# Three narrow products in place of one double-width and one narrow product, and gelu straight from the bank, in the expert up passes of a two-block transformer kernel

## The reference, cut to what matters

```
q = (x @ w_q).reshape(B, S, 8, 2, 128)
s = einsum('bshpk,hpnk->bshpn', q, sub_keys)          # scores of 2 x 128 sub-keys
top_s, top_i = top_k(s, 16); best_s, pos = top_k(cand_s, 16)
g = softmax(best_s);  ids = take_along_axis(cand_i, pos)
u = take(expert_u, ids);  act = gelu(einsum('td,tkd->tk', x, u)) * g
v = take(expert_v, ids);  out = einsum('tk,tkd->td', act, v)
h = x + out;  return rms_norm(h, final_norm_g)
```

## Time and profile before

| | |
|---|---|
| Time, median of 3 executions | 2957.54 us (2951.92 to 2960.43) |
| The profiled execution, its own time | 2955.81 us |
| Its span, first to last instruction | 2954.5 us |
| TensorE busy | 2911.7 us (99%) |
| VectorE busy | 2139.5 us (72%) |
| ScalarE busy | 1570.7 us (53%) |
| Mean granted TensorE clock | 0.997 of full |

### The profile page before, as it was taken

One profiled execution on the slowest core, in us unless ns is written; L12 is line 12 of the kernel. 1 busy time (PEld: TensorE's weight loads), 2 busy tenths in 40 slices (PEclk: granted clock), 3 DMA queues, 4 the chain that ended last, 5 costly groups with the idle time before them and its releaser, 6 DMA issues.

```text
span 2954.5 us, 45739 instructions
## 1 busy us (share of the span) xinstructions
PE 2911.7 (99%) x18502; PEld 2631.0 (89%) x18502; DVE 2139.5 (72%) x3352; ACT 1570.7 (53%) x2406; POOL 419.0 (14%) x304
## 2 busy tenths in 40 slices
PE   9999999999999999999998999999999999999998
PEld 7888888888888888899898999999999999999997
DVE  5566566666666455676589889778999777999776
ACT  4467755555555443577444556444556444556534
POOL 0011101111111000143020000232010133110131
PEclk9999999999999999999999999999999999999999
DMA  7544445555556554654564555788666788666784
GB/s 259 177 151 152 156 177 186 185 186 187 185 186 222 190 198 143 221 177 170 208 211 171 190 183 203 270 302 298 230 236 227 247 306 302 234 232 239 272 310 168
DMA packets 99009, 631.53 MB, mean 214 GB/s; under 512 B 11376, under 2 KB 12784, under 8 KB 31216
## 3 DMA queue, kind: packets, MB, share of 16 engines
q1 hardware_dynamic: 80368, 561.49, 54.3%
q0 software_dynamic: 18432, 67.12, 6.3%
HBM read 623.32 MB, written 4.19 MB: 212 GB/s over the span
## 4 chain that ended last, share of the span: by engine, by line
PE 78%; DMA 9%; DVE 8%; ACT 3%; issue 2%; SPq 0%; ACTq 0%; DVEq 0%
PE ps L292 26%; PE ps L293 13%; PE ps L1406 6%; PE ps L314 6%; PE ps L316 6%; PE ps L315 6%; DMA ring<-in_u_rows_dram,idx 5%; DMA ring<-in_v_rows_dram,idx 4%; PE ps L1408 3%; DVE loR L274 3%; PE ps L305 2%; PE ps L304 2%; PE ps L303 2%; ACT hiR L266 1%; PE ps L1311 1%
## 5 line engine op out<-in xcount | busy, mean ns | idle before, releaser
L274 DVE TENSOR_TENSOR loR<-raw,hiR 128x1024 fp32r<-128x1024 f32 x1017 | 1255.0, 1241 | 621.9 <-ACT hiR L266 618.4
L266 ACT CAST hiR<-raw 128x1024 fp32r<-128x1024 f32 x1026 | 1074.4, 1051 | 803.3 <-PE ps L1408 324.3
L292 PE MATMUL ps<-XA,hiR 128*128 128x448 f32 (+1 forms) x3936 | 1343.9, 391 | 10.7 <-DVE loR L274 9.3
L293 PE MATMUL ps<-XA,loR 128*128 128x224 f32 (+1 forms) x3936 | 1069.3, 272 | 0.0
L292 PEld LDWEIGHTS ps<-XA,hiR 128*128 128x128 f32 x3936 | 739.7, 188 | 127.1 <-DVE loR L274 6.6
L293 PEld LDWEIGHTS ps<-XA,loR 128*128 128x128 f32 x3936 | 747.7, 190 | 0.6
L1406 PE MATMUL ps<-hl,hiR 128*128 128x448 f32 x2048 | 651.0, 377 | 6.2 <-DVE loR L274 5.9
L1408 PE MATMUL ps<-hl,loR 128*128 128x224 f32 x2048 | 543.5, 265 | 0.0
L1406 PEld LDWEIGHTS ps<-hl,hiR 128*128 128x128 f32 x2048 | 385.2, 188 | 42.8 <-DVE loR L274 9.2
L1408 PEld LDWEIGHTS ps<-hl,loR 128*128 128x128 f32 x2048 | 392.1, 191 | 0.2 <-issue 0.2
L1447 POOL DMA_INDIRECT ring<-in_u_rows_dram,idx x64 | 103.2, 1612 | 716.8 <-DVE ring L1469 664.8
(11 more groups left out here) (307 smaller groups left out, 3490.1 us busy)
## 6 DMA issues: line engine op xcount, KB each, us to landing
raw<-in_u_dram SPq DMA_DIRECT2D x128, 1024.0 KB
raw<-in_v_dram SPq DMA_DIRECT2D x128, 1024.0 KB
raw<-in_w_up_dram SPq DMA_DIRECT2D x86, 1024.0 KB
raw<-in_w_down_dram SPq DMA_DIRECT2D x43, 1024.0 KB
raw<-in_w_in_qk_dram SPq DMA_DIRECT2D x32, 1024.0 KB
raw<-in_w_out_dram SPq DMA_DIRECT2D x32, 1024.0 KB
raw<-in_w_in_dram SPq DMA_DIRECT2D x24, 1024.0 KB
raw<-in_w_in_v_dram SPq DMA_DIRECT2D x16, 1024.0 KB
```

The source lines that it names most:

```text
L266: e.copy(hiR[:, r:r + 2, :], raw[n % NR][:, q:q + 2, :]).then_inc(S("hi"), 1)
L274: e.tensor_tensor(loR[:, r:r + 2, :], raw[n % NR][:, q:q + 2, :], hiR[:, r:r + 2, :].bitcast(F32), ALU.subtract).then_inc(S("lo_pool" if p ...
L292: e.matmul(both, wh, X.hl[:, :, k, 0:nt], start=(k == 0), stop=False, skip_group_check=True)
L293: m = e.matmul(dst[:, 0:nt], wl, X.h[:, k, 0:nt], start=False, stop=(k == KC - 1), skip_group_check=True)
```

## The change

A new function `narrow` takes the place of `wide` in the up passes of the experts: for each k three products of 224 columns, hi x h, hi x l, lo x h, into the first half of the bank. `act_u_part` and `dve_u_sum` are gone; `act_gelu` reads the bank and is placed where the copy was (s = 4i+5). TensorE waits for `s_gelu` where it waited for `u_sum`. Beside this some semaphores are merged (`sp_g` for three, `xsq` for two, `gp` for `gp` and `ident`). TS stays 32.

```diff
+    def narrow(e, g, q, X, dst, nt):
+        wait_piece(e, g)
+        hi, lo = hiR[:, g % NQ, :], loR[:, g % NQ, :]
+        for j in range(4):
+            k = 4 * q + j
+            wh, wl = hi[:, j * 128:(j + 1) * 128], lo[:, j * 128:(j + 1) * 128]
+            e.matmul(dst, wh, X.h[:, k, 0:nt], start=(k == 0), stop=False)
+            e.matmul(dst, wh, X.l[:, k, 0:nt], start=False, stop=False)
+            m = e.matmul(dst, wl, X.h[:, k, 0:nt], start=False, stop=(k == KC - 1))
+        m.then_inc(S("piece"), 1)
...
-    norm_load = [("gp", 16), ("g2", 16), ("ffn_const", 32), ("g5", 16)]
+    norm_load = [("gp", 32), ("g2", 16), ("ffn_const", 32), ("g5", 16)]
...
-            e.wait_ge(S("ident"), 16)
+            e.wait_ge(S("gp"), 32)
...
-    def act_u_part(e, r, s):
+    def act_gelu(e, r, s):
         i, left = divmod(s - 5, 4)
...
-        e.copy(S_[:, i, :], bank[u_of(r, i)][:, TD:2 * TD]).then_inc(S("u_part"), 1)
-
-    def dve_u_sum(e, r, s):
-        i, left = divmod(s - 6, 4)
...
-        e.wait_ge(S("u_part"), i0 + i + 1)
-        e.tensor_tensor(S_[:, i, :], S_[:, i, :], bank[u_of(r, i)][:, 0:TD], ALU.add).then_inc(S("u_sum"), 1)
-
-    def act_gelu(e, r, s):
-        i, left = divmod(s - 8, 4)
...
-        e.wait_ge(S("u_sum"), i0 + i + 1)
-        e.activation(S_[:, i, :], S_[:, i, :], ACT.Gelu_apprx_tanh).then_inc(S("s_gelu"), 1)
+        e.activation(S_[:, i, :], bank[u_of(r, i)][:, 0:TD], ACT.Gelu_apprx_tanh).then_inc(S("s_gelu"), 1)
...
                 if r == 0 and 4 <= i < FOUR + 2:
-                    e.wait_ge(S("u_sum"), i - 3)
+                    e.wait_ge(S("s_gelu"), i - 3)
                 elif i >= 2 and (r or i >= FOUR + 2):
-                    e.wait_ge(S("u_sum"), i0 + i - 1)
+                    e.wait_ge(S("s_gelu"), i0 + i - 1)
                 for q in range(4):
-                    wide(e, P_U[r] + 4 * i + q, q, XA, bank[u_of(r, i)], TD)
+                    narrow(e, P_U[r] + 4 * i + q, q, XA, bank[u_of(r, i)][:, 0:TD], TD)
...
-        load(e, "ident", ident[:, :], A["ident"])
+        load(e, "gp", ident[:, :], A["ident"])
```

More of the change, by code:

```diff
@@ L1340, in act_u_part @@
             e.wait_ge(S("sel"), 2)
-        e.copy(S_[:, i, :], bank[u_of(r, i)][:, TD:2 * TD]).then_inc(S("u_part"), 1)
-    def dve_u_sum(e, r, s):
-        i, left = divmod(s - 6, 4)
-        i0, i1 = RANGES[r]
-        if left or not 0 <= i < i1 - i0:
-            return
-        e.wait_ge(S("u_part"), i0 + i + 1)
-        e.tensor_tensor(S_[:, i, :], S_[:, i, :], bank[u_of(r, i)][:, 0:TD], ALU.add).then_inc(S("u_sum"), 1)
-    def act_gelu(e, r, s):
-        i, left = divmod(s - 8, 4)
-        i0, i1 = RANGES[r]
-        if left or not 0 <= i < i1 - i0:
-            return
-        e.wait_ge(S("u_sum"), i0 + i + 1)
-        e.activation(S_[:, i, :], S_[:, i, :], ACT.Gelu_apprx_tanh).then_inc(S("s_gelu"), 1)
+        e.activation(S_[:, i, :], bank[u_of(r, i)][:, 0:TD], ACT.Gelu_apprx_tanh).then_inc(S("s_gelu"), 1)
     def dve_gated(e, r, p):
@@ L1452, in act_rows @@
         if SLOT.get(s - 1) == NROW:
-            e.wait_ge(S("sp_dot"), 1)
-            e.activation(gated[:, :], gated[:, :], ACT.Gelu_apprx_tanh).then_inc(S("sp_gelu"), 1)
+            e.wait_ge(S("sp_g"), 1)
+            e.activation(gated[:, :], gated[:, :], ACT.Gelu_apprx_tanh).then_inc(S("sp_g"), 1)
     def dve_rows(e, s):
         if SLOT.get(s - 2) == NROW:
-            e.wait_ge(S("sp_gelu"), 1)
+            e.wait_ge(S("sp_g"), 2)
             e.wait_ge(S("sp_ix"), 2 + 3 * (128 // TS))
-            e.tensor_tensor(gated[:, :], gated[:, :], gs[:, :], ALU.mult).then_inc(S("sp_a"), 1)
+            e.tensor_tensor(gated[:, :], gated[:, :], gs[:, :], ALU.mult).then_inc(S("sp_g"), 1)
         m = row_of(s)
@@ L1471, in dve_rows @@
             elif j == 0:
-                e.wait_ge(S("sp_a"), 1)
+                e.wait_ge(S("sp_g"), 3)
                 e.tensor_scalar(vsum[:, cs], rg, gated[:, 0:1], None, ALU.mult).then_inc(S("sp_use"), 1)
@@ L1479, in dve_rows @@
             e.wait_ge(S("sp_use"), NROW)
-            e.tensor_tensor(gated[:, :], dots[:, :, 0], dots[:, :, 1], ALU.add).then_inc(S("sp_dot"), 1)
+            e.tensor_tensor(gated[:, :], dots[:, :, 0], dots[:, :, 1], ALU.add).then_inc(S("sp_g"), 1)
     Y_AT = [NI - 1 + 26 + (NI - 1) * f for f in range(3)]
@@ L1708, in pe_program @@
                 elif f == 1:
-                    e.wait_ge(S("u_sum"), i1)
+                    e.wait_ge(S("s_gelu"), i1)
                     e.wait_ge(S("g_ev"), NG * (r + 1))
@@ L1730, in act_program @@
         e.wait_ge(S("x0"), 16)
-        e.activation(tmp0[:, 0, :], x[:, 0, :], ACT.Square, accum_out=ss[:, 0:1]).then_inc(S("x0sq"), 1)
-        e.wait_ge(S("x0sq"), 1)
-        e.wait_ge(S("x1sq"), 1)
+        e.activation(tmp0[:, 0, :], x[:, 0, :], ACT.Square, accum_out=ss[:, 0:1]).then_inc(S("xsq"), 1)
+        e.wait_ge(S("xsq"), 2)
         act_root(e, 0, ss)
@@ L1827, in act_program @@
                     act_choice(e, 64 + s)
-                act_u_part(e, r, s)
                 act_gelu(e, r, s)
@@ L1835, in act_program @@
                 if s < 5:
-                    act_u_part(e, r, n + s)
                     act_gelu(e, r, n + s)
@@ L1879, in dve_program @@
         e.scalar_tensor_tensor(tmp0[:, 1, :], x[:, 1, :], 1.0, x[:, 1, :], ALU.mult, ALU.mult,
-                               accum_out=ss[:, 1:2]).then_inc(S("x1sq"), 1)
+                               accum_out=ss[:, 1:2]).then_inc(S("xsq"), 1)
         dve_root(e, 0, ss)
@@ L1974, in dve_program @@
                     dve_v_sum(e, r - 1, P_U[r] - P_VV[r - 1] + s)
-                dve_u_sum(e, r, s)
                 dve_gates(e, r, s)
@@ L1981, in dve_program @@
                 split_lo(e, P_VV[r] + s + LA)
-                if s < 4:
-                    dve_u_sum(e, r, n + s)
                 dve_gated(e, r, s)
```

## The result

The changed kernel takes 2989.36 us (2987.7 to 2993.15) against 2957.54: a ratio of 1.0114, 95% interval 1.0101 to 1.0128, about +34 us by the ratio and 31.8 between the medians, where +20.9 was forecast.

A forecast was written before the change was run, and what follows sets the result against it. TensorE's pace was taken to bind, except in 63 us of decoding where VectorE does. Products +27.4 and decoding stretch -6.5 gave +20.9 us: median 2978 us, 0.7% slower, range 2962 to 3002.

The forecast's parts named there:

- Three products of 224 columns: Up passes: 0.327 us a k from loads 0.109 apart, against 0.3136 for the pair; +27.4 us over 2048 k.
- bound (c): Twelve 128-column float32 weight loads in a row, short products not covering them: 0.112 us each, 0.336 a k, +45.9 us.
- The decoding stretch: 63 us starting up pass 0, experts' choice decoded, VectorE binding: 4.4 us relief, 2.1 of slower products hidden; -6.5 together.
- ScalarE's blocked queue: Decoding stretch: ScalarE stands 19.6 us in `act_gelu` for the sums, `split_hi` queued behind; expected to go in part.
- The drop of the clock: Decoding stretch: granted clock 0.97 over 63 us costs 1.9 us, counted only in the bound of about -13.
- the two bounds: Gelu reading the bank on ScalarE: taken as between the copy's 0.340 us and the present gelu's 0.392.
- Waits moved: TensorE's block start waits for the gelu at step 4i+5, not the sum at 4i+6; merged semaphores; cost 0.
- R1: Up passes: columns alone bound, 0.1067 us a product, +6.6 us in all, 2964 us; chance 0.13 together with R4.
- R2: Up passes: a 224-column product lets the next start after 0.10 us; -34 us, 2923 us; chance 0.07.
- R3: Up passes: loads have a pace of 0.120 us, 0.360 a k; +95.0 less some 8, 3045 us; chance 0.05.
- R4: Up passes: the second load of `wh` is skipped; in time it would be R1 or R2; 0.13 together with R1.
- R5: ScalarE reads the bank late and TensorE waits for `s_gelu`: +13 us on top, 2991 us; chance 0.03.

The follow-up runs named there:

- pace alone: Kernel before with the three narrow products, ScalarE's copy and VectorE's sum kept: 1.0126 (1.0100 to 1.0152) of the kernel before, median 2985.06 us.
- relief alone: Changed kernel with the double-width and narrow pair back, no copy, no sum, hi x l left out: 0.9978 (0.9960 to 0.9997) of the kernel before.

## Why the prediction was right, and which term was mis-sized

- **What bounds.** Right. TensorE's pace set the end of the steady up passes; that VectorE's share fell from 94% to 82% there moved nothing.
- **Three products of 224 columns.** The mechanism was right: each product loads its own weights, and it isn't the columns that set the pace. The widths 128, 192 and 224 with one step, and 256 with a longer one, show it. That it is the load, and not another fixed cost of an fp32r product, is argued from bound (c) of the prediction, and no run separates the two. It isn't a cost of every product with a load: the eight f16 gate products of the timeline above have all their loads within 0.27 us. The size was off: the step of 0.109 between two neighbouring loads of a pair was taken for the pace of a series. It is that of the first loads after a long product or a pause (0.110 over five); from there on it is 0.112, which bound (c) had given; the range held because it reached to (c). With 0.3356 a k in place of 0.327 the term is +45 us instead of +27.4.
- **The decoding stretch.** -6.5 was forecast; up pass 0 stayed 6.7 under its price. The parts came out otherwise: 3.6 us hidden (pace alone) and 3.0 given back (relief alone), where 2.1 and 4.4 stood in the sum; that the total fits so closely is luck. The waits on `loR` fell to 4.5, not to some 3. ScalarE's blocked queue seems to have been over-rated: its wait on the sum turned into waits for TensorE and for the exp's input. The drop of the clock went: the granted clock in the stretch is 1.00 after 0.97.
- **Copy and sum beside a full TensorE.** Worth 0 but for 1.7 us of waits at the start of up pass 1 that had been overlooked as small. The gelu from the bank takes 0.357 us, between the two bounds:

```profile
L1353 ACT ACTIVATE S__146<-ps x128: 352/357/360, 1571.1 to 2753.3; 128x224 f32<-128x224 f32 x128
```

- **Waits moved.** TensorE waited for the gelu 0.5 us in all. The start cost nothing: the first scaled norm begins at 11.00 us, after the reciprocal, as before at 11.12.
- **Down passes.** +1.8 us in the sum of three, from -5.1 to +4.7 in one: scatter of the size allowed for.
- **The sum.** 45.0 - 6.7 - 1.7 + 1.8 - 1.9, with rounding and the rest of up passes 1 and 2 (-0.8), gives the 35.7 of the spans. R1 and R2 are refuted by the steps, R3 by 0.112 against 0.120, R4 by the count of loads, R5 by TensorE's 0.5 us of waits for the gelu. Of the signs named, up pass 1 was to grow by 9.2 us and grew by 12.8.

The Trainium skill, "TensorE: Matmul & The Clock Gate", section on LDWEIGHTS, gives 107 ns for 128 columns. The widths from 128 to 224 show 0.112 in a series. An estimate of 6144 loads by the page's figure would be short by some 31 us.

## What to carry to other kernels

Count weight loads as well as columns. Here fp32r products of 128 to 224 columns, each with its load, came 0.112 us apart, and 0.120 at 256. Splitting a double-width product in two put twice 0.112 us in place of 0.205, though no column was added: the double-width product covers the load behind it, two narrow ones don't. And take a pace from a series: the first steps after a pause are faster than what follows. Work removed from an engine is worth only what it does where that engine binds, so look for that stretch first and price it alone.

## What the runs showed of the hardware beyond that

- With 128 columns, TensorE had gapless products at 1.2 GHz for 390 us and more of up pass 0 after one stall (0.50 granted, matmul and load busy 390.00 of 390 us), while the same products after a down pass ran at 1.00 throughout up pass 1. With 192, 224 and 256 columns no such stretch came (mean clock 0.998 in all three). One stall alone doesn't bring it about: the changed kernel waited six times for `loR` in that stretch, the longest also 1.3 us, at a granted clock of 1.00. No run here tells what decides.
- All four executions with 128 columns had a low mean clock, 0.932 or 0.933 in three, 0.87 in the one of 3385.37 us. But a kernel with wide products isn't free of it: of 17 executions of the kernel before one, that of 4798.73 us, had a mean clock of 0.606. Neither was profiled.
- At that level the step of loads was 0.213 us (three in 0.64), 1.9 times 0.112.
